# Expert weights of a hierarchical MoE layer loaded in 8 KB runs, with tokens transposed at a step of 16

## What is computed

```python
def hier_moe(v, w_coarse, w_fine, w_gate, w_up, w_down):
    t = v.reshape(-1, D)                                   # 400 x 2048
    ...                                                    # gates: 2 of 32 experts per token
    hg = jnp.einsum('td,edf->tef', t, w_gate)              # w_gate, w_up: 32 x 2048 x 256, float32
    hu = jnp.einsum('td,edf->tef', t, w_up)
    act = jax.nn.silu(hg) * hu * gates[:, :, None]
    out = jnp.einsum('tef,efd->td', act, w_down)           # w_down: 32 x 256 x 2048
```

## Time and profile before

| | us |
|---|---|
| Runs (lowest, median, highest) | 1904.34, 1904.63, 1913.32 |
| Span of the profiled execution, first to last instruction | 1909.7 |
| Experts, first token transpose to last down product | 1195 to 1835 |
| Busy over the whole span: PE, DVE, ACT, POOL | 1622.7, 1144.6, 806.0, 653.4 |

### The profile page before, as it was taken

The page is one execution under the profiler, slowest core; times in us unless marked ns, Lnnn a source line. Parts: engine busy times, 40 slices in busy tenths (PEclk is TensorE's granted clock), DMA queues, the critical chain, the costliest instruction groups (busy, mean ns, idle before and its releaser), DMA issues.

```text
span 1909.7 us, 23968 instructions
## 1 busy us (share of the span) xinstructions
PE 1622.7 (85%) x8404; PEld 1341.0 (70%) x8404; DVE 1144.6 (60%) x1402; ACT 806.0 (42%) x757; POOL 653.4 (34%) x931
## 2 busy tenths in 40 slices
PE   1989898797898899999999992899999999999920
PEld 1888887696887799999999992555555555555510
DVE  3661766866855764333242226577777777777726
ACT  3313222222222223222232234577777777766722
POOL 1007989987978700400001112122222222122102
PEclk9998988897987999999999996899999999999965
DMA  7432322222322334843442336699999999999835
GB/s 138 106 111 68 100 78 87 85 74 67 110 68 86 91 111 129 174 132 110 128 136 89 110 110 209 221 340 344 350 344 341 350 337 342 333 347 334 295 104 132
DMA packets 282535, 344.58 MB, mean 180 GB/s; under 512 B 27192, under 2 KB 262200, under 8 KB 278644
## 3 DMA queue, kind: packets, MB, share of 16 engines
q1 hardware_dynamic: 269848, 324.52, 54.5%
q0 software_dynamic: 7344, 17.34, 3.4%
q10 hardware_dynamic: 5272, 1.84, 0.4%
HBM read 337.28 MB, written 20.54 MB: 187 GB/s over the span
## 4 chain that ended last, share of the span: by engine, by line
PE 49%; DVE 19%; issue 11%; DMA 9%; ACT 8%; POOL 3%; SPq 0%; DVEq 0%; POOLq 0%; ACTq 0%
PE PS L928 31%; PE PS L1145 8%; DVE spL L1209 3%; ACT mHg L778 3%; DVE mLg L1643 3%; PE PS L1123 3%; DMA mraw_b<-w_up 2%; PE PS L947 2%; DVE work L1234 2%; DVE st L1235 2%; ACT yo L797 2%; DMA yk<-ybuf 2%; DVE work L1233 2%; ACT mHd L778 1%; DVE work L1231 1%
## 5 line engine op out<-in xcount | busy, mean ns | idle before, releaser
L928 PE MATMUL PS<-uHL,spH 128*128 128x400 f32 x2560 | 687.7, 351 | 15.6 <-DVE spL L1209 13.0
L928 PEld LDWEIGHTS PS<-uHL,spH 128*128 128x128 f32 x2560 | 482.5, 192 | 27.2 <-issue 13.6
L1209 DVE TENSOR_TENSOR spL<-raw,spH 128x2048 fp32r<-128x2048 f32 x100 | 232.5, 2325 | 359.2 <-ACT spH L571 358.5
L928 PE MATMUL PS<-uHL,spL 128*128 128x400 f32 x1280 | 447.7, 350 | 0.0
L571 ACT ACTIVATE spH<-raw 128x2048 fp32r<-128x2048 f32 x100 | 191.3, 1913 | 488.3 <-PE PS L928 466.6
L928 PEld LDWEIGHTS PS<-uHL,spL 128*128 128x128 f32 x1280 | 246.4, 192 | 0.1
L1123 PE MATMUL PS<-mHg,xTH 128*68 128x512 f32 x512 | 203.2, 397 | 1.8 <-issue 0.9
L1123 PE MATMUL PS<-mHg,xTL 128*68 128x512 f32 x512 | 202.0, 395 | 0.0
L1123 PE MATMUL PS<-mLg,xTH 128*68 128x512 f32 x512 | 201.4, 393 | 0.0
L1643 DVE TENSOR_TENSOR mLg<-mraw_a,mHg 128x2048 fp32r<-128x2048 f32 x65 | 146.0, 2289 | 44.8 <-ACT mHg L778 44.8
L1643 DVE TENSOR_TENSOR mLg<-mraw_b,mHg 128x2048 fp32r<-128x2048 f32 x63 | 141.9, 2289 | 36.4 <-ACT mHg L778 36.4
(11 more groups left out here) (290 smaller groups left out, 2380.3 us busy)
## 6 DMA issues: line engine op xcount, KB each, us to landing
raw<-w_in SPq DMA_DIRECT2D x64, 1024.0 KB, 5.9
mraw_a<-w_gate SPq DMA_DIRECT2D x33, 1024.0 KB, 10.1
mraw_b<-w_down SPq DMA_DIRECT2D x33, 1024.0 KB, 11.2
mraw_a<-w_up SPq DMA_DIRECT2D x32, 1024.0 KB, 11.3
mraw_b<-w_up SPq DMA_DIRECT2D x32, 1024.0 KB, 13.1
mraw_b<-w_gate SPq DMA_DIRECT2D x31, 1024.0 KB, 12.3
mraw_a<-w_down SPq DMA_DIRECT2D x31, 1024.0 KB, 10.8
raw<-w_o SPq DMA_DIRECT2D x16, 1024.0 KB, 5.4
```

The source lines that it names most:

```text
L928: ins = pe.matmul(PS[:, b + m, 0:T], PT[w][:, s, k * UW + m * P:k * UW + (m + 1) * P], rhs[:, a, k0 + k, :], start=first and k == 0 and (w ...
L1209: dve.tensor_tensor(spL[:, s, :], raw[:, s, :], spH[:, s, :].bitcast(F32), ALU.subtract).then_inc(lo_done, 1)
```

## The change

The rows of `w_gate` and `w_up` are renumbered: row = 16 p + 8 h + k instead of 128 k + p (h is the half, k runs from 0 to 7). Partition p of a tile then holds 8 rows that lie next to each other: one run of 8 KB. To match, chunk k of a token is no longer the features 128 k to 128 k + 127 but the features k, 16 + k, 32 + k and so on, so a transpose reads `xg` with a step of 16 floats (64 bytes). `w_down` is loaded by row block (rows 128 k to 128 k + 127, one run of 8 KB per partition) instead of by column half, and `down` loops over row blocks outside and over the four column blocks inside, with a wait for the DVE result of each row block instead of one wait for both.

```diff
-        w_gate_v = w_gate[0].rearrange("e (k p) n -> e p k n", p=P)
-        w_up_v = w_up[0].rearrange("e (k p) n -> e p k n", p=P)
+        w_gate_v = w_gate[0].rearrange("e (p h k) n -> e h p (k n)", h=2, k=UK)
+        w_up_v = w_up[0].rearrange("e (p h k) n -> e h p (k n)", h=2, k=UK)
...
-                sp.dma_start(mraw[s].rearrange("p (k c) -> p k c", k=k), src).then_inc(m_in[s], 16)
+                sp.dma_start(mraw[s], src).then_inc(m_in[s], 16)
 
             def load_gu(n, e, half):
-                mload(n, w_gate_v[e][:, half * UK:(half + 1) * UK, :], UK)
-                mload(n + 1, w_up_v[e][:, half * UK:(half + 1) * UK, :], UK)
+                mload(n, w_gate_v[e][half])
+                mload(n + 1, w_up_v[e][half])
 
             def load_d(n, e):
-                for h in range(2):
-                    mload(n + h, w_down_v[e][:, :, h * (D // 2):(h + 1) * (D // 2)], 2)
+                for k in range(2):
+                    mload(n + k, w_down_v[e][:, k, :])
...
                     for k in range(4):
                         ins = pe.transpose(PS[:, 2 + b % 2, k * CM:(k + 1) * CM],
-                                           xg[0:CM, (4 * b + k) * P:(4 * b + k + 1) * P], ident[0:CM, 0:CM])
+                                           xg[0:CM, :].rearrange("c (p k) -> c k p", k=KD)[:, 4 * b + k, :],
+                                           ident[0:CM, 0:CM])
                     ins.then_inc(xg_tr, 1)
...
             def down(e, n0):
                 pe.wait_ge(al_done, e + 1)
                 ge(pe, yo_done, e)
-                pe.wait_ge(mlo, n0 + 2)
-                for c in range(4):
-                    for k in range(2):
+                for k in range(2):
+                    pe.wait_ge(mlo, n0 + 1 + k)
+                    for c in range(4):
                         for w, a in PASSES:
-                            o = k * (D // 2) + (c % 2) * 512
-                            ins = pe.matmul(PS[0:CM, 4 + c, :], AT[a][:, k, :], MD[w][:, c // 2, o:o + 512],
+                            ins = pe.matmul(PS[0:CM, 4 + c, :], AT[a][:, k, :], MD[w][:, k, c * 512:(c + 1) * 512],
                                             start=k == 0 and (w, a) == (0, 0), stop=k == 1 and (w, a) == PASSES[-1])
                 ins.then_inc(dn_done, 1)
```

More of the change, by code:

```diff
@@ L470, in _, with mload @@
             cursor = [0]
-            def mload(n, src, k):
+            def mload(n, src):
                 s = cursor[0] % MRAW
@@ L523, in _ @@
                         sp.wait_ge(o_ye, n + 1)
-                        sp.dma_start(ogu[:, 0], w_gate_v[e]).then_inc(o_w, 16)
-                        sp.dma_start(ogu[:, 1], w_up_v[e]).then_inc(o_w, 16)
+                        sp.dma_start(ogu[:, 0].rearrange("p (h k) n -> p h (k n)", h=2),
+                                     w_gate_v[e].rearrange("h p m -> p h m")).then_inc(o_w, 16)
+                        sp.dma_start(ogu[:, 1].rearrange("p (h k) n -> p h (k n)", h=2),
+                                     w_up_v[e].rearrange("h p m -> p h m")).then_inc(o_w, 16)
                         sp.dma_start(odn[:, :, :], w_down_v[e]).then_inc(o_w, 16)
@@ L1175, in _ @@
                         ins = pe.transpose(PS[:, 2 + k // 4, (k % 4) * CM:(k % 4 + 1) * CM],
-                                           xg[0:CM, k * P:(k + 1) * P], ident[0:CM, 0:CM])
+                                           xg[0:CM, :].rearrange("c (p k) -> c k p", k=KD)[:, k, :],
+                                           ident[0:CM, 0:CM])
                     ins.then_inc(o_tr, 1)
```

## The result

The changed kernel takes 1942.88 us (median of four runs, 1937.96 to 1944.04), the kernel before, run beside it, 1907.91 us. The ratio is 1.0167 with a 95% interval of 1.0142 to 1.0193. Forecast were 1904.5 us with a range of 1890 to 1926; the time lies above it, and the cause was none of the four rivals.

What follows compares the result with a forecast made beforehand. PE was taken to set the 19.14 us beat, with DMA right beside it and nothing left over. Terms of -8.5, -2.2 and +10.6 summed to -0.1 us against the 1904.63 us median: 1904.5 us, range 1890 to 1926.

Steps and rivals of the forecast that it cites:

- 8 KB runs: Gate, up and down loads: longer runs let loads finish ahead of the beat, removing three breaks; -8.5 us.
- three breaks: Late among the experts: the beat breaks three times on a gate-or-up load of 15.5 to 15.9 us; 8.5 us lost.
- Transposes at a step of 64 bytes: PE's sixteen token transposes per expert: the strided read makes each 0.040 us longer; +10.6 us.
- d: Extra time per strided token transpose on PE; 26 to 40 ns, upper end taken.
- The first eight: First half of an expert's token transposes: their extra time is hidden up to about 0.7 us.
- PE's gap: PE's wait for DVE between the two halves of the token transposes; 1.18 us, said to stay.
- 264 d: Exposed cost of strided transposes: second eight in 31 experts plus the first expert's sixteen; +10.6 us.
- Down products by row block: Last expert: the first 12 down products start after DVE's first tile split instead of both; -2.2 us.
- B: Rival: dear strided reads hold up down products and the whole beat; 1936 us, or 1917 at 87 ns; chance 0.17.
- A: Rival: the strided read in the transposes is free; 1893.9 us, chance 0.26.
- C: Rival: longer runs don't speed the loads, so the breaks stay; 1913.0 us, chance 0.04.
- D: Rival: long runs make loads slower, 4.6 us more than the beat per expert; 2045 us, chance 0.03.

Runs made afterwards that it cites:

- plain_transposes: The changed kernel with all sixteen token transposes of an expert reading contiguous columns again; 1905.16 us, ratio 0.9985 to the kernel before.
- split_1kb: The kernel before (1 KB runs, contiguous transposes) with its first twelve down products between the two halves of the token transposes; 1908.61 us, ratio 0.9982.
- perm_split: The changed kernel with features reordered once by ACT, contiguous transposes, and twelve down products between the token transposes' halves; 1858.55 us, ratio 0.9717.
- gap_filled: The changed kernel with four unread products per expert, from the second on, in PE's gap between the token transposes' halves; 1913.47 us, ratio 1.0014.
- plain_wait: The changed kernel with contiguous transposes and a longer wait for DVE before the second eight; 1945.06 us, ratio 1.0171.
- step_12: The changed kernel with the last four of an expert's sixteen transposes contiguous, twelve keeping the step; 1923.38 us, ratio 1.0077.
- step_only: The kernel before with only the step of 16 in the transposes, keeping 1 KB runs and the old down order; 1936.14 us, ratio 1.0128.
- plain_32: The changed kernel with 32 contiguous transposes per expert, each of the sixteen done twice into the same place; 1921.91 us, ratio 1.0056.

## Why the prediction was wrong

- **8 KB runs.** Right in kind: packets and the three breaks came out as said. That the queue's share of 84.7% lies in the forecast 79 to 85% is luck: the slow beats stretched the window, and in undisturbed beats it is 89.0% (`plain_transposes`). The rate per engine was 22.7 GB/s, under the 24.2 to 26.0 that I took; the margin was enough for it. The Trainium skill, "DMA: Bandwidth & Descriptors", section "Specifications", gives line rate from 512 bytes on; `split_1kb` against `perm_split`, 20.5 and 24.3 GB/s per engine, disagrees with it too. The size of the term, 8.5 us, held in the profiled execution (experts 9.2 us shorter in `plain_transposes`) but not in the medians (3.8). I had read it from one execution; runs of the kernel before spread from 1900 to 1920 us. Nor was all of it waiting for loads, as the lines under the step that failed show.
- **Transposes at a step of 64 bytes.** The price was nearly right: from the second eight's start to the first down product 1522.16 - 1521.24 = 0.92 us where the earlier trace rows give 0.55, so d = 0.37 / 8 = 46 ns against 40. That it came so near is partly luck, as the 40 was carried over from rows of another engine, of which the one at 291 ns reads PSUM and the one at 378 ns SBUF. The Trainium skill, "SBUF — State Buffer", section "Door 1: The DMA port swizzle", lets a step of four floats pass free and has a penalty beyond, without its size; the trace agrees that a step of 16 floats costs time, and the half rate that the prediction assumed for it gave 45 ns. The first eight were hidden, as said: the second eight start 1.83 us after the first, before 1.84. PE's gap, which the prediction had at 1.18 us as before, shrank for the same reason to 0.85 us. The term measures 264 x 46 ns = 12.1 us against 10.6.
- **The step that failed** is the one that set this term down as its own time only, 264 d, with every matmul at the price of the earlier trace rows. What the slower transposes do to the clock was put at nothing. I had read the granted clock of 1.00 in the earlier trace rows and taken it as given. The slower transposes are also time in which PE is held up, beside a gap of 1.18 us that was there already, and with both the clock falls at the down products behind them: 28 us, more than twice the term itself. `gap_filled` shows it from one side, `plain_wait` from the other. Rows of the kernel before could have warned me: behind the three load breaks, where PE waits 1.8 to 2.2 us between the transposes instead of 1.18, its own down products took 7.10, 6.66 and 8.07 us.

```profile
1618.36 7.10 PE PS L1145 x24
...
1678.38 6.66 PE PS L1145 x24
...
1757.29 8.07 PE PS L1145 x24
```

Against 3 x 5.53 that is 5.2 us more: of the 8.5 us that I had put down to late loads, 3.3 were waiting and 5.2 were the slow products behind it.

- **Down products by row block.** Sized at -2.2 us, measured -0.4: the products start 1.0 us earlier and take 0.6 us longer. I followed the wait for DVE's second split and didn't ask what is late next: ACT has to evict the products of the expert before from the same PSUM banks, and does that behind its own rounding. That is read from the chain; no run was made on it.
- **The rivals.** The sign was B's, but its mechanism wasn't: the undisturbed beat is 19.51 us, inside the bounds that I had set for the forecast. A's case, transposes at no extra cost, is `plain_transposes`: 1905.2 us and not 1893.9, part of which is the base, as the kernel before gave 1908 to 1911 us beside the experiments and not 1904.63. C and D fell with the loads.

Open is in which beats the clock falls: 12 to 20 of 30 with the same instructions in each, and the count seems to differ between runs (`step_12` ran from 1908 us, at a mean clock of 0.924, to 1935 us, at 0.915). The order isn't quite without rule: in `plain_wait` two slow groups and a fast one alternate, and in the changed kernel and `step_only` no two fast groups behind token transposes follow one another. Whether a held-up transpose and an empty wait count alike can't be told from these runs.

## What to carry to other kernels

Where PE stops for a microsecond in every beat, look at the granted clock of the products behind the stop, and price anything that makes the stop longer with these products at the lower clock as well; 0.27 us more per beat cost 40 us here. Better, put products with ready operands into the gap, and do a renumbering where it is paid once; and check that the loads can follow before closing a gap, since a faster layout shows its worth only when something else no longer sets the beat.

## What was not expected of the hardware

- The same beat, with the same gap and the same instructions, ran at 19.51 us or at 21.08 us: the clock fell in some beats and stayed in others.
- A longer stretch of transposes at full pace did no harm to the clock, a longer wait did: 0.27 us more in the gap brought 20 slow groups (`plain_wait`), a stretch 0.46 us longer with twice the transposes and a shorter wait none (`plain_32`).
- ACT's fp32 copy of 2048 elements reads at a step of 64 bytes in 3.74 us instead of 1.99, 1.9 times as long; PE's weight load of 128 columns costs 46 ns more on 69 with the same step, 1.7 times.
- Loads of 8 KB runs moved 22.7 GB/s per engine in the mix of the beat, 24.3 where nothing but PE held the beat (`perm_split`), and not the 26.0 that a load by itself showed.
